# Forgetting attention in three steps a head instead of four: the first two query tiles share a step

## The chip, the cores and the metric

The kernel runs on one core of a Trainium2 chip. The metric is the device time of one execution in microseconds (us), lower is better. Engines are named as in the profile: PE is TensorE's matmul stream and PEld its weight loads, DVE is VectorE, ACT is ScalarE, POOL is GpSimd, and SPq is the SyncE queue that issues most transfers. Engines run side by side, each through its own instructions strictly in order, and wait for each other on semaphores.

## The reference, cut to what matters

The program is one step of a hybrid decoder: a combined projection, four branches (A to D), a merge, cross-attention over a memory and a feed-forward part, for 512 prompt tokens and 8 single-token samples. The change touches branch D for the prompt alone: causal attention with a forget gate, 8 heads of width 64, 512 queries in four tiles of 128.

```python
ck = jnp.swapaxes(c_k, 1, 2)[:, :, None, :]          # c = cumsum(log f)
def block(args):                                      # one tile of 128 queries
    qi, ci, pi = args
    s = jnp.einsum('bqhd,bkhd->bhqk', qi, k, preferred_element_type=F32) * (d ** -0.5)
    s = s + jnp.swapaxes(ci, 1, 2)[..., None] - ck
    s = jnp.where(k_pos[None, None, None, :] <= pi[None, None, :, None], s, NEG_INF)
    p = jax.nn.softmax(s, axis=-1)
    return jnp.einsum('bhqk,bkhd->bqhd', p.astype(v.dtype), v)
```

Query tile q sees q + 1 blocks of 128 keys, so its logits are 128, 256, 384 or 512 columns wide for q = 0 to 3. For the samples the same branch reads 128 pages of 256 KB of cached values (`cache_fox_v`), which is work of its own beside the prompt's.

## The kernel before, in words

All large products run as "pieces": 128 output columns of a weight matrix by all 520 tokens, in two halves of 260 tokens (`h` = 0 and 1). A half piece is 24 PE instructions (8 blocks of contraction, 3 products each for precision) or, for the `br` kinds (branch outputs, contraction 512), 12. Everything else is hung between half pieces. The function `timeline` writes one list of events for all engines, and each engine walks it and does its part of every event:

- `("piece", p, h)`: PE's half piece. With h = 0, SP issues the weights of piece p + 4, ACT and then POOL or DVE split those of piece p + 2 in a high and a low part.
- `("side", K, s)`: one step of the list `SIDE`, exactly one after each half piece, unless a `BEFORE` mark makes `through` put all steps up to that mark out in a row.
- `("evac", m)`: the finished tile m is taken out of PSUM by ACT or DVE.
- `("v", g)` and `("vx", b)`: a group of four cached value pages, multiplied on PE (`v_group`), and after each fourth group the sum over heads (`v_heads`), which needs a product that DVE makes first (L2067, waiting for the group) and a copy by DVE after it (L2071). At `("v", g)` SP issues the four pages of group g + 1 once group g - 1 has been used. `("PAGES",)` puts out all groups still open, one behind the other.

An attention step `("fox", n)` is a stage of a pipeline over n. Its PE part computes the logits of tile n into bank s0, transposes the exponentials of tile n - 1 into s1, and multiplies those of tile n - 2 with V into s2. Its DVE part, which comes first, takes the row maximum of tile n - 1's logits (L1790) and divides the result of tile n - 3 by its row sum (the reciprocal L1795, then a product recorded at L1599). Its ACT part copies the transposes out (L1380) and makes the exponentials (L1388), after DVE's maximum. Before PE starts its part of step n it waits until DVE and ACT have finished theirs of step n (L967 and L969); DVE and ACT wait for PE's part of step n - 1. So a step's DVE work is hidden only as far as PE has a half piece or a value group to run between its parts of step n - 1 and n:

```python
                done = K if kind == "y" else K + 1
                if upto(act_works, done):
                    pe.wait_ge(act_s.sem, upto(act_works, done))
                if upto(dve_works, done):
                    pe.wait_ge(dve_s.sem, upto(dve_works, done))
```

Pieces 82 to 95 (kinds `brB`, `gateB`) and 96 (`gateD`) run beside these steps. Before piece 97 the mark `("BEFORE", "brD")` puts out all attention steps and value groups that are left, then `("df", 1)`, which finishes the samples' part of branch D. After that `("split", "brD")` lets ACT write the high part of the branch's result (`oh`), and six export steps `("ex", n)` and the load of the cross-attention memory (`ml`) follow.

Of the kernel before, what the change touches and what calls it, by code (L numbers as in the profile page):

```python
# [18 lines left out]
ACT = mybir.ActivationFunctionType  # L19
AX = mybir.AxisListType.X  # L20
MUL, ADD, SUB, MAX, MIN = ALU.mult, ALU.add, ALU.subtract, ALU.max, ALU.min

P = 128
# [5 lines left out]
QT = SEQ // P  # L29
# [4 lines left out]
FH, FD = 8, 64  # L34
# [122 lines left out]
    return max(p for p, x in enumerate(PIECES) if x[3] == kind)  # L157


FOX = 4 * FH  # L160
XU = QT * XH // 2
VG = 4

# [283 lines left out]
def build(nc, a, out):  # L447
    ctx = ExitStack()
    with ctx:
# [25 lines left out]
        OD, OB, OC, QKV, G, DEC = 0, 2080, 4160, 6240, 12480, 18624  # L475
        DEC_N = 4 * 512 + 512 + PAGES * NB * FH
        SQ = DEC + DEC_N
# [6 lines left out]
        def v(at, *shape):  # L484
            n = int(np.prod(shape))
            x = ar[:, at:at + n]
            if len(shape) == 2:
                x = x.rearrange("p (a b) -> p a b", a=shape[0])
            if len(shape) == 3:
                x = x.rearrange("p (a b c) -> p a b c", a=shape[0], b=shape[1])  # L490
            return x

        oD, oB, oC = v(OD, KB, T), v(OB, KB, T), v(OC, KB, T)
        qkv = v(QKV, 12, T)
        fq, fk, fv = oD, qkv[:, 4:8, :], qkv[:, 8:12, :]
# [30 lines left out]
        bias = small(20)  # L526
        eps6, eps5 = small(1), small(1)
        dcol, edc, edl, kdf, bed = (small(16) for _ in range(5))
        nmx, rsum = small(2), small(2)
# [13 lines left out]
        s0, s1, s2, s3 = (sd[:, n, :] for n in range(4))  # L543
# [16 lines left out]
        pool_c, act_c, dve_c = stage("pool_chain"), stage("act_chain"), stage("dve_chain")  # L560
# [5 lines left out]
        pe_s, act_s, dve_s = stage("pe_side"), stage("act_side"), stage("dve_side")  # L566
        v2a, a2v = stage("dve_to_act"), stage("act_to_dve")
# [30 lines left out]
        wsl = nc.alloc_sbuf_tensor_at("wsl", [P, KD, 16], F32R, offset=base + 4 * (G + 256))  # L598
        zrow = v(G + 1024, T)
        vt = v(G, QT, 4 * 192)  # L600
        fP, fPT, frs = v(G + 3072, 512), v(G + 3584, QT, P), v(SQ, P)
        stg = v(G + 4096, 2, 512)

        cnh = nc.alloc_sbuf_tensor_at("cnh", [P, 512], F32R, offset=base + 4 * (G + 5632))
# [36 lines left out]
        def sel(h):  # L641

            return mask_r[0:NB, 0, h:h + 1].to_broadcast([NB, P])
# [190 lines left out]
        def _(pe):  # L834
            def mm(o, l, r, start=True, stop=True):
                return pe.matmul(o, l, r, start=start, stop=stop, skip_group_check=True)  # L836
# [114 lines left out]
            def side(K, s):  # L951
# [60 lines left out]
                    last = mm(s1[:, 32:64], cs(I_HI), f)  # L1012
                elif kind == "fox":
                    if n < FOX:
                        h, q = divmod(n, QT)
                        r = slice(FD * (h % 2), FD * (h % 2) + FD)
                        w = (q + 1) * P
                        mm(s0[:, 0:w], fq[r, h // 2, q * P:(q + 1) * P], fk[r, h // 2, 0:w], True, False)
                        mm(s0[:, 0:w], sel(h), cnh[0:FH, 0:w], False, False)
                        mm(s0[:, 0:w], sel(h), cnl[0:FH, 0:w], False, False)  # L1020
                        last = mm(s0[:, q * P:w], mask_r[:, 0, :], mask_r[:, 1, :], False, True)
                    if 1 <= n <= FOX:
                        for b in range((n - 1) % QT + 1):
                            last = tr(s1[:, b * P:(b + 1) * P], fP[:, b * P:(b + 1) * P])
                    if 2 <= n <= FOX + 1:
                        h, q = divmod(n - 2, QT)
                        for b in range(q + 1):
                            last = mm(s2[:, 0:P], vt[:, b, 192 * (h // 2) + FD * (h % 2):192 * (h // 2) + FD * (h % 2) + 2 * FD], fPT[:, b, :], b == 0, b == q)
                elif kind == "l2p":
                    for j in range(2):  # L1030
                        for h in range(2):
# [156 lines left out]
        def _(act):  # L1188
# [118 lines left out]
            def side(K, s):  # L1307
# [8 lines left out]
                fins = None  # L1316
# [58 lines left out]
                elif kind == "fox":  # L1375
                    if n == 1:
                        act.wait_ge(ss_st, 32)
                    w = ((n - 2) % QT + 1) if 2 <= n <= FOX + 1 else 1
                    if 2 <= n <= FOX + 1:
                        fins = act.activation(fPT[:, 0:w, :], s1[:, 0:w * P].rearrange("p (a b) -> p a b", a=w), ACT.Copy)  # L1380
                    else:
                        fins = act.activation(rsum[:, 1:2], eps6[:, 0:1], ACT.Copy)
                    if n <= FOX:
                        act_c.by(fins)
                        w = ((n - 1) % QT + 1) * P
                        act.wait_ge(v2a.sem, va + 1)
                        act.wait_ge(act_c.sem, act_c.n)
                        fins = act.activation(fP[:, 0:w], s0[:, 0:w], ACT.Exp, bias=nmx[:, 0:1])  # L1388
                elif kind == "l2":
                    if n == 0:  # L1390
                        act.wait_ge(qs_out, 16)
# [201 lines left out]
        def _(dve):  # L1593
            def own(ins, st=dve_c):
                st.by(ins)
                dve.wait_ge(st.sem, st.n)

            def tt(o, x, y, op, st=dve_c):
                own(dve.tensor_tensor(o, x, y, op), st)  # L1599
# [136 lines left out]
            def side(K, s):  # L1736
# [49 lines left out]
                    tt(cnl[0:FH, :], cneg[0:FH, :], cnh[0:FH, :].bitcast(F32), SUB, dve_s)  # L1786
                elif kind == "fox":
                    if n <= FOX:
                        w = ((n - 1) % QT + 1) * P
                        v2a.by(dve.tensor_reduce(nmx[:, 0:1], s0[:, 0:w], AX, MAX, negate=True))  # L1790
                    if n >= 3:
                        h, q = divmod(n - 3, QT)
                        r = slice(FD * (h % 2), FD * (h % 2) + FD)
                        rs_ = slice(FD - FD * (h % 2), 2 * FD - FD * (h % 2))
                        own(dve.reciprocal(frs[r, :], s2[rs_, 0:P]))  # L1795
                        tt(oD[r, h // 2, q * P:(q + 1) * P], s2[r, 0:P], frs[r, :], MUL, dve_s)
                    else:
                        fin()
                elif kind == "l2":
# [307 lines left out]
```

## Time and profile before

| | before |
|---|---|
| median of 3 runs | 1736.78 us (1733.03 to 1740.67) |
| the profiled execution, its own time | 1732.22 us |
| its span, first to last instruction | 1729.2 us |
| PE busy, share of the span | 1486.3 us, 86% |
| DVE, ACT, POOL busy | 961.7, 556.1, 563.1 us |
| mean granted TensorE clock | 0.923 of full speed |

PE is the engine that works most, and most of what it does is pieces; the attention steps and value groups between 805 and 1029 us are a part in which it also waits. All positions are microseconds from the start of the span. The granted clock is a share of full speed (1.00 is 2.4 GHz, 0.50 is 1.2 GHz).

### The profile page before, as it was taken

How to read it: one execution, taken by the hardware profiler on the slowest of the kernel's cores; microseconds unless marked ns; L12 is line 12 of the kernel's file. 1: busy time of each engine (PE TensorE's matmuls, PEld its weight loads, DVE VectorE, ACT ScalarE, POOL GpSimd, SP SyncE). 2: the span in 40 equal slices, each digit the busy share in tenths (PEclk: the TensorE clock that was granted, in tenths of full speed). 3: DMA queues.
4: the chain of work that ended last, by engine and by line, in shares of the span. 5: the costliest groups of instructions: out<-in, count | busy, mean ns of one | idle time of the engine just before them, and what ended most of it. 6: DMA issues, size and time to landing. Idle time of an engine off the chain costs nothing. (4 is left out here: it accounts for less than half of the span.)

```text
span 1729.2 us, 28170 instructions
## 1 busy us (share of the span) xinstructions
PE 1486.3 (86%) x11055; PEld 1379.2 (80%) x11055; DVE 961.7 (56%) x1366; ACT 556.1 (32%) x858; POOL 563.1 (33%) x311
## 2 busy tenths in 40 slices
PE   5986878688887989789888879898669999999995
PEld 5886877688887989766666658898558999999995
DVE  3189896899968675533223332265246777772212
ACT  5322650212133222534222222355335223233222
POOL 3355453343442433011111103320504444443440
PEclk9988987899998999999888889999879999999997
DMA  7425432434442544258444436433323333332331
GB/s 201 130 68 145 118 115 68 131 90 116 123 128 86 147 116 129 68 164 256 125 134 134 128 103 201 130 86 103 127 69 104 89 95 95 90 98 71 101 92 50
DMA packets 254643, 199.83 MB, mean 116 GB/s; under 512 B 15780, under 2 KB 212957, under 8 KB 254104
## 3 DMA queue, kind: packets, MB, share of 16 engines
q1 hardware_dynamic: 234149, 169.47, 34.0%
q10 hardware_dynamic: 19371, 23.86, 4.2%
q0 software_dynamic: 992, 4.72, 0.8%
q8 instruction: 87, 1.43, 0.3%
q14 instruction: 44, 0.36, 0.1%
HBM read 187.89 MB, written 10.81 MB: 115 GB/s over the span
## 5 line engine op out<-in xcount | busy, mean ns | idle before, releaser
L836 PE MATMUL pb<-xh,wh 128*128 128x260 f32 x2176 | 642.0, 295 | 34.1 <-ACT ar L1195 16.6
L836 PE MATMUL pb<-xl,wh 128*128 128x260 f32 x2176 | 628.7, 289 | 0.0
L836 PE MATMUL pb<-xh,rawl 128*128 128x260 f32 x2176 | 627.1, 288 | 0.0
L790 POOL TENSOR_TENSOR rawl<-raw,wh 128x1024 fp32r<-128x1024 f32 (+2 forms) x152 | 343.9, 2263 | 859.1 <-ACT wh L1195 858.5
L836 PEld LDWEIGHTS pb<-xh,wh 128*128 128x128 f32 x2176 | 425.1, 195 | 42.0 <-issue 28.7
L836 PEld LDWEIGHTS pb<-xl,wh 128*128 128x128 f32 x2176 | 425.3, 195 | 0.5
L836 PEld LDWEIGHTS pb<-xh,rawl 128*128 128x128 f32 x2176 | 424.7, 195 | 0.0
L1195 ACT ACTIVATE wh<-raw 128x1024 fp32r<-128x1024 f32 (+2 forms) x208 | 201.6, 969 | 513.1 <-PE pb L836 463.3
L836 PE MATMUL sd<-ar 128*128 128x128 f32 (+7 forms) x1488 | 258.8, 390 | 95.9 <-DVE ar L1599 63.3
L836 PEld LDWEIGHTS sd<-ar 128*128 128x128 f32 (+4 forms) x1488 | 177.2, 192 | 141.5 <-issue 85.0
L805 POOL TENSOR_TENSOR ar<-ar 128x512 f32<-128x512 f32 x128 | 191.1, 1493 | 249.0 <-DMA ar<-in_cache_fox_k 226.7
L836 PE MATMUL pb<-oh,wh 128*128 128x260 f32 (+1 forms) x384 | 120.6, 314 | 7.4 <-ACT ar L1195 5.4
L1727 DVE SCALAR_TENSOR_TENSOR ar<-xT,cols,ar 128x512 f32<-128x512 f32 x120 | 125.2, 1081 | 1.2
L836 PE MATMUL pb<-ol,wh 128*128 128x260 f32 (+1 forms) x384 | 114.5, 298 | 0.0
L836 PE MATMUL pb<-oh,rawl 128*128 128x260 f32 (+1 forms) x384 | 114.3, 298 | 0.0
L1710 DVE TENSOR_TENSOR rawl<-raw,wh 128x1024 fp32r<-128x1024 f32 (+1 forms) x56 | 67.1, 1199 | 75.4 <-ACT wh L1195 75.3
L840 PE MATMUL sd<-cst,ar 128*128 128x128 f32 (+6 forms) x363 | 63.7, 291 | 48.9 <-ACT ar L1505 20.7
L836 PE MATMUL pb<-hh,wh 128*128 128x260 f32 x352 | 100.0, 284 | 2.6 <-DVE hl L1599 2.6
L836 PE MATMUL pb<-hh,rawl 128*128 128x260 f32 x352 | 99.5, 283 | 0.0
L836 PE MATMUL pb<-hl,wh 128*128 128x260 f32 x352 | 99.3, 282 | 0.0
L1619 DVE SCALAR_TENSOR_TENSOR ar<-ar,cols 128x512 f32<-128x512 f32 x88 | 96.7, 1099 | 4.2 <-ACT ar L1195 2.6
L1734 DVE TENSOR_REDUCE ar<-ar 128x8 f32<-128x512 f32 x128 | 85.0, 679 | 23.1 <-POOL ar L805 22.1
(193 smaller groups left out, 1693.0 us busy)
## 6 DMA issues: line engine op xcount, KB each, us to landing
raw<-in_w_in SPq DMA_DIRECT2D x80, 512.0 KB, 4.2
ar<-in_cache_fox_k SPq DMA_DIRECT2D x128, 256.0 KB, 2.7
ar<-in_cache_fox_v SPq DMA_DIRECT2D x128, 256.0 KB, 3.1
raw<-in_w_ffn_in SPq DMA_DIRECT2D x44, 512.0 KB, 3.7
raw<-in_w_branch SPq DMA_DIRECT2D x32, 256.0 KB, 3.2
raw<-in_w_ffn_out SPq DMA_DIRECT2D x16, 512.0 KB, 3.9
ar<-in_cache_mem_k ACTq DMA_DIRECT2D x1, 4096.0 KB, 19.7
raw<-in_w_out SPq DMA_DIRECT2D x8, 512.0 KB, 3.9
```

The source lines that it names most:

```text
L790: pool.tensor_tensor(rawl[:, p % RING, 0:kt, :], raw[:, p % RING, 0:kt, :], wh[:, p % (AHEAD + 1), 0:kt, :].bitcast(F32), SUB).then_inc(lo ...
L805: own(pool.tensor_tensor(kring[:, i % 4, :], kring[:, i % 4, :], qb[:, :], MUL), prod_done)
L836: return pe.matmul(o, l, r, start=start, stop=stop, skip_group_check=True)
L840: return pe.transpose(o, i, ident[0:n, 0:n])
L1195: own(act.activation(o, i, f, **kw), st)
L1619: (st if j == width - 2 else dve_c).by(dve.scalar_tensor_tensor(out=y[:, 0:SEQ], in0=x[:, 4 - width + j:4 - width + j + SEQ], scalar=wcol( ...
L1710: dve.tensor_tensor(rawl[:, p % RING, 0:kt, :], raw[:, p % RING, 0:kt, :], wh[:, p % (AHEAD + 1), 0:kt, :].bitcast(F32), SUB).then_inc(lo. ...
L1727: dve_c.by(dve.scalar_tensor_tensor(out=oC[:, c, 0:SEQ], in0=g[:, j - 1:j - 1 + SEQ], scalar=w[:, j - 1:j], in1=oC[:, c, 0:SEQ], op0=MUL, ...
L1734: page_free.by(dve.tensor_reduce(sc[:, i, :], kring[:, i % 4, :].rearrange("p (h d) -> p h d", h=FH), AX, ADD))
```

## The change

Query tiles 0 and 1 (128 and 256 keys, together 384 columns) are put side by side in bank s0 and go through one step; tiles 2 and 3 keep a step each. A head takes three steps, and there are 27 attention steps in place of 35. The two tiles keep a row maximum and an exponential each; their three transposes are copied out at once; their results lie side by side in s2 (256 columns), and one reciprocal and one product, twice as wide, divide them.

```diff
-FOX = 4 * FH
+FOX = 3 * FH
+FOX_Q = ((0, 1), (2,), (3,))
+
+
+def fox_blocks(n):
+
+    return [(j, q, b) for j, q in enumerate(FOX_Q[n % 3]) for b in range(q + 1)]
...
-        fP, fPT, frs = v(G + 3072, 512), v(G + 3584, QT, P), v(SQ, P)
+        fP, fPT, frs = v(G + 3072, 512), v(G + 3584, QT, P), v(SQ, 2 * P)
...
-                        h, q = divmod(n, QT)
+                        h, at = n // 3, 0
                         r = slice(FD * (h % 2), FD * (h % 2) + FD)
-                        w = (q + 1) * P
-                        mm(s0[:, 0:w], fq[r, h // 2, q * P:(q + 1) * P], fk[r, h // 2, 0:w], True, False)
...
+                        for q in FOX_Q[n % 3]:
+                            w = (q + 1) * P
+                            o = s0[:, at:at + w]
+                            mm(o, fq[r, h // 2, q * P:(q + 1) * P], fk[r, h // 2, 0:w], True, False)
+                            mm(o, sel(h), cnh[0:FH, 0:w], False, False)
+                            mm(o, sel(h), cnl[0:FH, 0:w], False, False)
+                            last = mm(s0[:, at + q * P:at + w], mask_r[:, 0, :], mask_r[:, 1, :], False, True)
+                            at += w
                     if 1 <= n <= FOX:
-                        for b in range((n - 1) % QT + 1):
+                        for b in range(len(fox_blocks(n - 1))):
                             last = tr(s1[:, b * P:(b + 1) * P], fP[:, b * P:(b + 1) * P])
...
+                        for i, (j, q, b) in enumerate(fox_blocks(n - 2)):
+                            last = mm(s2[:, j * P:(j + 1) * P], vt[:, b, vs], fPT[:, i, :], b == 0, b == q)
...
+                        for j, q in enumerate(FOX_Q[(n - 1) % 3]):
+                            w = (q + 1) * P
+                            if j:
+                                act_c.by(fins)
+                            fins = act.activation(fP[:, at:at + w], s0[:, at:at + w], ACT.Exp, bias=nmx[:, j:j + 1])
+                            at += w
...
-                        w = ((n - 1) % QT + 1) * P
-                        v2a.by(dve.tensor_reduce(nmx[:, 0:1], s0[:, 0:w], AX, MAX, negate=True))
+                        qs, at = FOX_Q[(n - 1) % 3], 0
+                        for j, q in enumerate(qs):
+                            w = (q + 1) * P
+                            (v2a if j == len(qs) - 1 else dve_c).by(
+                                dve.tensor_reduce(nmx[:, j:j + 1], s0[:, at:at + w], AX, MAX, negate=True))
+                            at += w
                     if n >= 3:
-                        h, q = divmod(n - 3, QT)
+                        h, qs = (n - 3) // 3, FOX_Q[n % 3]
+                        w = len(qs) * P
...
-                        own(dve.reciprocal(frs[r, :], s2[rs_, 0:P]))
-                        tt(oD[r, h // 2, q * P:(q + 1) * P], s2[r, 0:P], frs[r, :], MUL, dve_s)
+                        own(dve.reciprocal(frs[r, 0:w], s2[rs_, 0:w]))
+                        tt(oD[r, h // 2, qs[0] * P:qs[0] * P + w], s2[r, 0:w], frs[r, 0:w], MUL, dve_s)
```

No half piece, value group or export step is added or taken away, and PE's products are the same ones. The list of events is the same up to the event `("v", 26)` behind piece 96, h = 0; what differs before it is only which tiles a step n handles. Behind it the order changes. PE's instructions from there to piece 97, before (`8x512` are the value groups, `128x1` their sums over heads, `sd<-cst,ar 128x128` transposes, `sd<-ar 128x128` the products with V, `pb` the pieces):

```order
4514 L836 MATMUL sd<-ar 8x512 x4
4515 L836 MATMUL sd<-ar 128x128
4516 L836 MATMUL sd<-cnh,mask_r 128x128
4517 L836 MATMUL sd<-cnl,mask_r 128x128
4518 L836 MATMUL sd<-mask_r 128x128
4519 L840 MATMUL sd<-cst,ar 128x128 x4
4520 L836 MATMUL sd<-ar 128x128 x3
4521 L836 MATMUL sd<-cst,ar 128x1 x4
4522 L836 MATMUL sd<-ar 128x256
4523 L836 MATMUL sd<-cnh,mask_r 128x256
```

This is value group 27, attention step 28, the sum over heads and the start of step 29; steps 30 to 33 with value groups 28 to 31 between them follow, and then piece 97. In the changed kernel PE has this between the two halves of piece 96 (the first two rows end half 0, the last two begin half 1):

```order
4498 L842 MATMUL pb<-xl,wh 128x260
4499 L842 MATMUL pb<-xh,rawl 128x260
4500 L842 MATMUL sd<-ar 8x512 x8
4501 L842 MATMUL sd<-cst,ar 128x1 x4
4502 L842 MATMUL sd<-ar 8x512 x16
4503 L842 MATMUL sd<-cst,ar 128x1 x4
4504 L842 MATMUL pb<-xh,wh 128x260
4505 L842 MATMUL pb<-xl,wh 128x260
```

All attention steps stand ahead of it, and value groups 26 to 31 stand in a row with nothing between them. On DVE, around the copy behind a sum over heads (step 12, beside piece 88), before:

```order
610 L2071 COPY ar<-sd 128x4
611 L1790 TENSOR_REDUCE ar<-sd 128x1
612 L1795 RECIPROCAL ar<-sd 64x128
613 L1599 TENSOR_TENSOR ar<-sd,ar 64x128
614 L1790 TENSOR_REDUCE ar<-sd 128x1
```

and in the changed kernel:

```order
610 L2091 COPY ar<-sd 128x4
611 L1808 TENSOR_REDUCE ar<-sd 128x1
612 L1815 RECIPROCAL ar<-sd 64x256
613 L1614 TENSOR_TENSOR ar<-sd,ar 64x256
614 L1808 TENSOR_REDUCE ar<-sd 128x1 x2
```

Steps whose number is a multiple of three now carry the wide reciprocal and product, and the step behind each carries two maxima.

## Rows read from the trace of the kernel before

Rows of stretches give: from:to and length in us; busy us and instructions of PE, PEld, DVE, ACT and POOL; the granted clock; the DMA share and GB/s. Timeline rows give start, length, engine, line and instruction, in brackets the idle time before and what ended it. Groups give count, busy us, mean ns of one, idle us before.

**Rows 1.** Stretches: steps beside pieces, the tail, and one slow stretch

```profile
805.30:989.20 183.90, 163.84 (x980) 123.39 (x984) 59.07 (x104) 40.89 (x74) 25.33 (x14) 0.84 0.46 136
989.20:1029.30 40.10, 30.76 (x169) 18.52 (x168) 13.04 (x22) 7.06 (x14) 1.26 (x1) 0.79 0.43 126
913.00:930.00 17.00, 14.66 (x63) 12.93 (x63) 4.91 (x10) 2.99 (x6) 2.45 (x2) 0.60 0.02 5
```

**Rows 2.** Who waited for whom from 805.3 to 1029.3 us: total, times, longest

```profile
PE sd L836 <- DVE ar L1599: 26.1, 12, 2.9
```

**Rows 3.** Timeline, two steps that PE waited for: behind a value group, behind sums

```profile
913.29 0.76 PE L836 MATMUL sd<-ar 64*128 64x128 f32 x2 [2.88 <-DVE ar L1599]
...
922.67 0.74 PE L836 MATMUL sd<-ar 64*128 64x256 f32 x2 [2.05 <-DVE ar L1599]
```

**Rows 4.** Groups of DVE instructions by shape: count, busy us, mean ns, idle before

```profile
L1795 DVE RECIPROCAL ar<-sd 64x128 f32<-64x128 f32 x32 | 30.6, 955 | 3.6 <-PE sd L836 2.6
L1599 DVE TENSOR_TENSOR ar<-sd,ar 64x128 f32<-64x128 f32 x32 | 9.2, 289 | 1.1
L1790 DVE TENSOR_REDUCE ar<-sd 128x1 f32<-128x512 f32 x8 | 5.5, 689 | 19.3 <-PE sd L836 19.3
L1790 DVE TENSOR_REDUCE ar<-sd 128x1 f32<-128x384 f32 x8 | 4.5, 558 | 23.4 <-PE sd L836 23.4
L1790 DVE TENSOR_REDUCE ar<-sd 128x1 f32<-128x256 f32 x8 | 3.4, 422 | 16.9 <-PE sd L836 14.3 <-PE sd L840 2.6
L1790 DVE TENSOR_REDUCE ar<-sd 128x1 f32<-128x128 f32 x8 | 2.3, 290 | 15.5 <-PE sd L836 15.4
...
L1950 DVE RECIPROCAL ar<-ar 128x64 f32<-128x64 f32 x1 | 0.6, 552 | 0.0
```

**Rows 5.** PE's part of a step, one stretch for each width, and the last step

```profile
900.60:902.50 1.90, 1.90 (x12) 1.06 (x9) 0.00 (x0) 0.32 (x1) 1.51 (x1) 1.00 0.64 195
905.10:907.70 2.60, 2.60 (x15) 1.42 (x12) 0.00 (x0) 0.00 (x0) 0.00 (x0) 1.00 0.77 215
942.00:944.00 2.00, 2.00 (x19) 1.78 (x16) 0.00 (x0) 0.00 (x0) 1.21 (x1) 1.00 0.90 227
948.00:950.20 2.20, 2.20 (x18) 1.69 (x15) 0.00 (x0) 0.00 (x0) 0.00 (x0) 1.00 0.35 111
1025.30:1026.50 1.20, 1.20 (x13) 1.06 (x9) 0.00 (x0) 0.00 (x0) 0.00 (x0) 0.90 0.00 0
```

**Rows 6.** Timeline, a step that hides behind a half piece and a value group

```profile
860.29 0.29 DVE L1790 TENSOR_REDUCE ar<-sd 128x1 f32<-128x128 f32 x1 [2.58 <-PE sd L836]
...
862.54 0.29 PEld L836 LDWEIGHTS sd<-ar 64*128 64x128 f32 x2 [0.86 <-issue]
```

**Rows 7.** Timeline of PE, from value group 25 to piece 97

```profile
979.46 0.67 PE L836 MATMUL sd<-ar 64*128 64x256 f32 x2 [0.41 <-DVE ar L1599]
...
983.20 1.89 PE L836 MATMUL sd<-ar 128*8 128x512 f32 x10
...
989.16 2.10 PE L836 MATMUL sd<-ar 128*8 128x512 f32 x10
...
995.76 1.04 PE L836 MATMUL sd<-ar 128*8 128x512 f32 x8
...
1001.79 1.71 PE L836 MATMUL sd<-cst,ar 128*128 128x1 f32 x8
...
1029.34 0.37 PE L836 MATMUL pb<-xh,wh 128*128 128x260 f32 x1
```

**Rows 8.** Value pages: SP's timeline (start, length, issues), and from issue to landing

```profile
976.21 3.63 SPq L728 DMA_DIRECT2D ar<-in_cache_fox_v  x4
...
985.01 35.44 SPq L728 DMA_DIRECT2D ar<-in_cache_fox_v  x20
...
ar<-in_cache_fox_v SPq DMA_DIRECT2D x93, 256.0 KB, 3.0
```

**Rows 9.** Timeline of ACT behind the last attention step

```profile
1031.63 2.65 ACT L1195 ACTIVATE oh<-ar 128x520 fp32r<-128x520 f32 x4 [3.48 <-DVE cols L1608]
```

More of the change, by code:

```diff
@@ L1014, in side @@
                     if n < FOX:
-                        h, q = divmod(n, QT)
+                        h, at = n // 3, 0
                         r = slice(FD * (h % 2), FD * (h % 2) + FD)
-                        w = (q + 1) * P
-                        mm(s0[:, 0:w], fq[r, h // 2, q * P:(q + 1) * P], fk[r, h // 2, 0:w], True, False)
-                        mm(s0[:, 0:w], sel(h), cnh[0:FH, 0:w], False, False)
-                        mm(s0[:, 0:w], sel(h), cnl[0:FH, 0:w], False, False)
-                        last = mm(s0[:, q * P:w], mask_r[:, 0, :], mask_r[:, 1, :], False, True)
+                        for q in FOX_Q[n % 3]:
[6 more added lines that the diff above has]
+                            at += w
                     if 1 <= n <= FOX:
-                        for b in range((n - 1) % QT + 1):
+                        for b in range(len(fox_blocks(n - 1))):
                             last = tr(s1[:, b * P:(b + 1) * P], fP[:, b * P:(b + 1) * P])
                     if 2 <= n <= FOX + 1:
-                        h, q = divmod(n - 2, QT)
-                        for b in range(q + 1):
-                            last = mm(s2[:, 0:P], vt[:, b, 192 * (h // 2) + FD * (h % 2):192 * (h // 2) + FD * (h % 2) + 2 * FD], fPT[:, b, :], b == 0, b == q)
+                        h = (n - 2) // 3
+                        vs = slice(192 * (h // 2) + FD * (h % 2), 192 * (h // 2) + FD * (h % 2) + 2 * FD)
+                        for i, (j, q, b) in enumerate(fox_blocks(n - 2)):
+                            last = mm(s2[:, j * P:(j + 1) * P], vt[:, b, vs], fPT[:, i, :], b == 0, b == q)
                 elif kind == "l2p":
@@ L1377, in side @@
                         act.wait_ge(ss_st, 32)
-                    w = ((n - 2) % QT + 1) if 2 <= n <= FOX + 1 else 1
+                    w = len(fox_blocks(n - 2))
                     if 2 <= n <= FOX + 1:
@@ L1384, in side @@
                         act_c.by(fins)
-                        w = ((n - 1) % QT + 1) * P
                         act.wait_ge(v2a.sem, va + 1)
                         act.wait_ge(act_c.sem, act_c.n)
-                        fins = act.activation(fP[:, 0:w], s0[:, 0:w], ACT.Exp, bias=nmx[:, 0:1])
+                        at = 0
+                        for j, q in enumerate(FOX_Q[(n - 1) % 3]):
[4 more added lines that the diff above has]
+                            at += w
                 elif kind == "l2":
@@ L1788, in side @@
                     if n <= FOX:
-                        w = ((n - 1) % QT + 1) * P
-                        v2a.by(dve.tensor_reduce(nmx[:, 0:1], s0[:, 0:w], AX, MAX, negate=True))
+                        qs, at = FOX_Q[(n - 1) % 3], 0
[4 more added lines that the diff above has]
+                            at += w
                     if n >= 3:
-                        h, q = divmod(n - 3, QT)
+                        h, qs = (n - 3) // 3, FOX_Q[n % 3]
+                        w = len(qs) * P
                         r = slice(FD * (h % 2), FD * (h % 2) + FD)
                         rs_ = slice(FD - FD * (h % 2), 2 * FD - FD * (h % 2))
-                        own(dve.reciprocal(frs[r, :], s2[rs_, 0:P]))
-                        tt(oD[r, h // 2, q * P:(q + 1) * P], s2[r, 0:P], frs[r, :], MUL, dve_s)
+                        own(dve.reciprocal(frs[r, 0:w], s2[rs_, 0:w]))
+                        tt(oD[r, h // 2, qs[0] * P:qs[0] * P + w], s2[r, 0:w], frs[r, 0:w], MUL, dve_s)
                     else:
```

## The prediction

> **What bounds the kernel now.** I read the busy shares of the page first, then PE's timeline of branch D. Over the whole program PE is the engine that works most, and wherever pieces run back to back nothing but PE's work counts. The attention steps lie in one part, which I cut in two: from step 0's start at 805.3 us to value group 26 at 989.2 us, where a half piece stands between any two steps, and the tail from there to piece 97 at 1029.3 us, where apart from the second half of piece 96 none does [rows 1]. PE has 20.1 us of idle time in the first stretch and 9.3 us in the tail, and runs at a mean clock of 0.84 and 0.79 in them. The table of waits says who it waits for: 26.1 us in 12 waits for DVE's product that ends a step [rows 2]. These waits are not spread evenly. All but a few stand behind a fourth value group (DVE must first do its head product, L2067, and only then the step) or behind a sum over heads (DVE's copy L2071 first). Two of them are 2.88 and 2.05 us [rows 3]. In all other steps a half piece and mostly a value group hide DVE: in one of them DVE starts at 860.29 and PE at 862.54, with PE never idle [rows 6]. So PE's time here is its own work, plus the waits at fixed places, plus a slower clock behind such waits (0.60 from 913 to 930 us [rows 1]). The number of steps as such costs PE next to nothing.
>
> **The change, part by part.** Between the start of step 0 and value group 26 there are 27 half pieces in either kernel, and a step after each but the last. Before, these slots take steps 0 to 26 of the 34 that have PE work; in the changed kernel they take all (0 to 25). I work out five terms.
>
> A, work moved into the first stretch. PE's part of a step took 2.0, 2.2, 1.9 and 2.6 us for steps whose number leaves 0, 1, 2 and 3 after division by four (the stretches from 942, 948, 900 and 905 us [rows 5]). Steps 27 to 33 go forward: 2.6 + 2.0 + 2.2 + 1.9 + 2.6, and the last two, without logits, 1.2 each (the last of [rows 5], for both). That is 13.7 us more before value group 26, and nothing hides it, since PE is what sets the pace there. I count no saving for eight fewer steps: the PE instructions are the same, and the slots between pieces remain.
>
> B, DVE's longer chain where PE already waits. A step's DVE work is the maximum of the tile before (0.29, 0.42, 0.56 or 0.69 us), a reciprocal of 0.955 and a product of 0.289 [rows 4]. The wide reciprocal of 256 is in no row. It can't be below the 0.96 of 128 columns nor, by proportion, above 1.91; between 64 and 128 columns the reciprocal grew by 0.403, 6.3 ns a column, which gives 0.955 + 128 x 0.0063 = 1.76, and I take that. The product of 256 I take as 0.42, adding the 0.13 that a maximum grows by from 128 to 256 columns [rows 4]. Going through the eight stalled steps of this stretch (5, 6, 10, 12, 16, 17, 22, 23) with the tiles that they now handle: steps 6 and 12 have the wide pair, where PE waits 1.2 and 0.95 us longer; steps 10, 16 and 22 get the two maxima of the merged tiles (0.29 + 0.42 + a gap of 0.03, for 0.42, 0.69, 0.42): 0.3, 0.05 and 0.3; steps 5 and 17 get 384 columns for 128: 0.27 each; step 23 stays. Sum 3.4 us. Queued behind the waiting PE step are the half piece and the value group after it, so all of this counts.
>
> C, steps that were hidden. With 12 instructions of a `br` half piece and a value group, PE came to its next step 2.25 us after DVE had begun, so some 2.1 us of DVE work fit [rows 6]; without the group's 1.04 us [rows 7] it is 1.2. The wide chain is 0.69 + 1.76 + 0.42 and gaps = 2.9 us. It sits in such a slot in steps 9 and 15: 0.8 us each. Step 18 has a `br` half piece alone: 1.8 us at full clock, less if the slow clock behind step 17 stretches the half piece; I take 1.2. Step 25 loses its maximum, as no logits come before it, and with it the wait of 0.41 us that it had [rows 7]. Steps 3 and 21 have 24 instructions and a group before them, 24 behind the slow clock; they stay hidden. Sum 2.4 us. The doubled exponential stays behind DVE's reciprocal and costs nothing; if it didn't, it would be the sum of two short ACT operations against one, under half a microsecond in each of eight steps.
>
> D, the tail. It took 40.2 us (989.16 to 1029.34 [rows 7]). In the changed kernel no step is left there, but neither is what hid the value pages. A group's four pages are issued 1.10 us apart ((3.63 - 0.34) / 3, if an issue itself takes 0.34 [rows 8]), so 4.4 us a group, and the last lands 3.0 us after its issue [rows 8]. Let value group 26 start at 0. Group 25 then started at -4.0: 1.04 for itself and 3.0 for the half piece, which is what 983.20 to 989.16 leaves beside the group and a step of 1.9 [rows 5, 7]. Group 27's pages are issued 1.8 us after that start (985.01 against 983.20 [rows 7, 8]), at -2.2, and land at 4.1. Groups 28, 29, 30 and 31 are issued from 2.2, 6.6, 11.0 and 15.4 on, by SP's pace alone, and land 3 x 1.10 + 3.0 = 6.3 later: 8.5, 12.9, 17.3, 21.7. Group 31 takes PE 1.04 us at full clock [rows 7] and, as the waits leave PE idle most of the time, likely nearly twice that, 1.9. DVE's head product over 512 columns (some 0.7, like a maximum of that width [rows 4]) with its hand-over, 1.0, and the sum over heads, 1.7 [rows 7], end the row at 26.3. The second half of piece 96 follows, 3.0 us at full clock and 6.0 at half; starting at half, 4.7. That is 31.0 us; at full clock throughout it is 21.7 + 1.0 + 1.0 + 1.0 + 3.0 = 27.7. I take 31.0: minus 9.2 us. The 13.7 of A leave the tail, but 4.5 of it comes back as waiting for pages.
>
> E, behind the tail. Before, piece 96 was complete ahead of the tail, so ACT had taken its tile out by the time piece 97 began, and started the four `oh` parts, 2.65 us together, 2.3 us after that [rows 7, 9]. Now piece 96 ends only behind the tail, and taking out its tile and the 2.65 stand between its end and ACT's first export copy, which PE's second export step needs, with one half piece of 3.0 for cover. I put 1.5 us, between 0 and 2.5.
>
> The sum: 13.7 + 3.4 + 2.4 - 9.2 + 1.5 = 11.8 us. The profiled execution took 1732.2 us of its own time with a span of 1729.2, so it would be 1744.0. That execution lies 4.6 us under the median of the runs shown, 1736.8; on the median the sum gives 1748.6, and I forecast 1748. About 0.5% or 8.7 us is what a measurement of this kernel can tell from no change: 1728.1 to 1745.5.
>
> **A rule weighed.** The Trainium skill (VectorE: DVE Perf Modes, on the TRN2 errata) says that VectorE pays a fixed cost per instruction and that one large tile pays it once where many small ones pay each. The maxima agree: 290 ns for 128 columns and 689 for 512 leave 157 ns that don't depend on width [rows 4]. By that rule alone 16 fewer instructions save 2.5 us and the kernel would come out 2.5 us faster, 1734. The saving is real on DVE, which is 56% busy; PE waits for it only at the places above, and there the merged step puts more in one wait and less in another, with both inside B and C.
>
> **The rivals.** (1) Little of B and C is seen and the tail runs at full clock: that is 13.7 + 3.4 + 0 - 12.5 + 0 = 4.6 us, 1741, no change that can be told. For it: the tail's clock rose again at times (group 27 took 1.04 at 995.76 [rows 7]). Against: pages come only every 4.4 us there. (2) The slow clock goes away, and the kernel is faster. The first stretch lost 0.16 of 183.9 us to the clock, 29 us, of which some 5 fell on idle time [rows 1]. Denser steps behind a wait (2.8 us of PE work on average for 2.2) could bring TensorE back to 2.4 GHz sooner. To reach minus 0.5% it must give back 11.8 + 8.7 = 20.5 of those 24 us; with all of them the time is 1725. Against it: the waits before the slow stretches do not get shorter, two of them grow by about 1 us. (3) The reverse: the new waits of 0.8 to 1.2 us in steps 9, 15 and 18 fall into stretches that ran at 2.4 GHz and pull the clock to 1.2 there. Three stretches of 5 us more at half clock cost 7.5 us: 1756. For it: such a wait stands one or two steps before one of 3 us. Against: the wait of 0.41 us at 979.46 changed nothing. (4) If the time hung on the number of steps, eight fewer at their mean distance of 6.6 us (224.0 us for 34 steps) would save 53 us; the slots without PE idle time speak against it, and I give it nothing of its own.
>
> The Trainium skill (TensorE: Matmul & The Clock Gate, Part 1) has the clock fall after idle time of PE and return after sustained work. By this rule the tail with 20 us of sparse value groups runs at the low level; the trace agrees so far as 913 to 930 us lay behind waits.
>
> **How the numbers follow.** The forecast gets 0.54, with a range of its own of 1743 to 1755: from D's full clock and E at 0 (plus 7.0) to wide reciprocals of 1.91 in six waits (0.9), E at 2.5 (1.0) and 4 us more of slow clock (plus 17.7). Rival 1 gets 0.23, rival 3 0.13, rival 2 0.10. The range of 1735 to 1758 leaves out rival 2 and the upper part of rival 3. Slower by over 0.5%: four fifths of the forecast's case, all of rival 3 and a little of rival 1, 0.58. Within 0.5%: 0.32. Faster: 0.10.
>
> **What would show it.** A: 26 steps of mean 2.8 us PE work before value group 26, and that group some 19 us later after step 0's start than the 183.9. B and C: reciprocals of 64x256 near 1.76 us; waits near 3.4 us at steps 6 and 12 and near 0.8 at 9 and 15. D: value groups 28 to 31 about 4.4 us apart, each ended by a DMA wait, and 31 us from group 26 to piece 97. E: a wait of PE for ACT's copy before the second export step. It would be wrong if the half-clock stretches shrank, if pages landed faster than SP's pace, or if PE's part of a merged step were shorter than the two it replaces.

## The result and the profile after

The changed kernel is slower: 1758.13 us, median of 4 runs (1755.49 to 1759.28), against 1737.0 us for the kernel before beside it; the ratio is 1.0122, 95% interval 1.0103 to 1.0142. That is 21 us. The profiled execution took 1757.97 us of its own time, 25.8 more than that of before. From the page of the changed kernel, the span and the busy times of the engines:

```profile
span 1756.2 us, 28112 instructions
PE 1508.7 (86%) x11055; PEld 1390.2 (79%) x11055; DVE 959.9 (55%) x1350; ACT 553.7 (32%) x850; POOL 560.6 (32%) x311
```

PE has the same 11055 instructions and is busy 22 us longer: most of the loss is PE's own work done more slowly, not waits. The stretches of the changed kernel that answer to [rows 1] (step 0 to value group 26; the tail to piece 97; piece 97 to the place in the order of pieces where the row of before below ends):

```profile
804.70:1016.80 212.10, 186.65 (x1060) 138.34 (x1064) 65.30 (x105) 44.48 (x78) 25.30 (x14) 0.82 0.40 116
1016.80:1044.90 28.10, 23.15 (x93) 6.99 (x93) 4.38 (x13) 0.07 (x1) 0.00 (x0) 0.94 0.61 182
1044.90:1078.70 33.80, 26.95 (x192) 25.93 (x190) 8.49 (x13) 12.17 (x22) 7.93 (x5) 0.85 0.56 185
```

and the kernel before in the third of them, which was not needed for the prediction:

```profile
1029.30:1056.40 27.10, 23.61 (x194) 22.35 (x194) 8.65 (x20) 11.10 (x20) 7.89 (x4) 1.00 0.46 149
```

The first stretch grew by 28.2 us (183.90 to 212.10), the tail shrank by 12.0 (40.10 to 28.10), and the part behind it grew by 6.7 (27.10 to 33.80). That is 22.9 of the 27.0 us between the two spans (1756.2 - 1729.2); the rest is 4.7 us behind these stretches and 0.6 less ahead of them, where the kernels are the same. In the first stretch PE's idle time went from 20.1 us (183.90 - 163.84) to 25.4 (212.10 - 186.65), 5.4 more. The other 22.8 are busy time, and the same stretch cut by output tile shows whose (`pb` are the pieces; `sd` the attention steps and value groups). Before, `pb` first and `sd` second:

```profile
805.30:989.20 183.90, 75.14 (x480) 70.17 (x480) 5.57 (x8) 3.62 (x6) 0.84 0.46 136
805.30:989.20 183.90, 98.22 (x500) 56.05 (x504) 47.31 (x86) 25.26 (x53) 0.84 0.46 136
```

After, in the same order:

```profile
804.70:1016.80 212.10, 74.91 (x480) 70.22 (x480) 4.87 (x7) 3.62 (x6) 0.82 0.40 116
804.70:1016.80 212.10, 121.24 (x580) 70.87 (x584) 55.41 (x89) 28.66 (x56) 0.82 0.40 116
```

(The two overlap in time, so they add up to more than PE's busy time.) The pieces cost the same in sum, the steps and groups 23.0 us more. The 80 PE instructions moved in were priced at 13.7 us at full clock, which leaves 9 us. The granted clock has two levels, so a mean of 0.84 says that 2 x 0.16 x 183.9 = 59 us were at the lower one, and 0.82 over 212.1 us that 76 were. Seventeen us more at half clock cost some 8.5 us of busy time, by this estimate nearly all of the 9. The waits of PE in the changed kernel from 804.7 to 1078 us (in total, times, longest), to set beside [rows 2]:

```profile
PE sd L842 <- DVE ar L1614: 25.4, 11, 3.4
PE sd L846 <- DMA ar<-in_mem_prompt: 3.6, 1, 3.6
PE sd L846 <- ACT ar L1480: 3.1, 2, 2.3
PE sd L842 <- DMA ar<-in_cache_fox_v: 2.9, 6, 1.2
```

The wait for DVE's product is as large as before in sum, but all of it now stands in the first stretch (before it was 20.0 us in 9 waits there). The waits for the value pages are new, and those for ACT's export copy are longer: before they are 0.61 and 0.51 us, at the third and the fifth export step. DVE's groups, beside [rows 4]:

```profile
L1815 DVE RECIPROCAL ar<-sd 64x128 f32<-64x128 f32 x16 | 15.3, 955 | 2.9 <-PE sd L842 2.4
L1815 DVE RECIPROCAL ar<-sd 64x256 f32<-64x256 f32 x8 | 14.0, 1756 | 0.2
...
L1614 DVE TENSOR_TENSOR ar<-sd,ar 64x256 f32<-64x256 f32 x8 | 3.4, 422 | 0.3
```

Both sizes that no row of before had came out as estimated (1.76 and 0.42 us).

Two places in PE's timeline of the changed kernel, steps 15 and 16 and then step 18, show what the added waits do:

```profile
923.50 0.46 PE L842 MATMUL sd<-ar 64*128 64x128 f32 x2 [0.76 <-DVE ar L1614]
...
926.13 1.08 PE L846 MATMUL sd<-cst,ar 128*128 128x128 f32 x4
927.00 1.49 PE L842 MATMUL sd<-ar 128*128 128x128 f32 x6
928.14 0.57 PE L842 MATMUL pb<-oh,wh 128*128 128x260 f32 x1
...
931.02 1.47 PE L842 MATMUL sd<-ar 128*8 128x512 f32 x8
935.30 0.95 PE L842 MATMUL sd<-ar 64*128 64x384 f32 x1 [2.82 <-DVE ar L1614]
...
954.61 0.46 PE L842 MATMUL sd<-ar 64*128 64x128 f32 x2 [1.25 <-DVE ar L1614]
...
957.60 1.07 PE L846 MATMUL sd<-cst,ar 128*128 128x128 f32 x4
958.47 1.49 PE L842 MATMUL sd<-ar 128*128 128x128 f32 x6
959.61 0.57 PE L842 MATMUL pb<-xh,wh 128*128 128x260 f32 x1
```

Step 15 waits 0.76 us, and its PE part, from 923.50 to 928.14, takes 4.6 us; the half piece of 12 behind it, to 931.02, takes 2.9, where 1.6 is its time at full clock. Step 18 waits 1.25 us and takes 5.0. A merged step's PE part takes 3.3 us where the clock is full, as in step 9 of this kernel. The tail, PE's timeline again, beside [rows 7]:

```profile
1016.77 1.04 PE L842 MATMUL sd<-ar 128*8 128x512 f32 x8
1019.04 3.01 PE L842 MATMUL sd<-ar 128*8 128x512 f32 x8 [1.22 <-DMA ar<-in_cache_fox_v]
...
1037.96 1.85 PE L842 MATMUL sd<-ar 128*8 128x512 f32 x4 [0.24 <-DMA ar<-in_cache_fox_v]
1040.67 1.05 PE L842 MATMUL sd<-cst,ar 128*128 128x1 f32 x8 [0.85 <-DVE ar L2087]
1041.58 0.36 PE L842 MATMUL pb<-xh,wh 128*128 128x260 f32 x1
...
1044.55 0.60 PE L846 MATMUL sd<-cst,ar 128*11 128x128 f32 x4
...
1050.33 0.61 PE L846 MATMUL sd<-cst,ar 128*11 128x128 f32 x4 [2.30 <-ACT ar L1480]
...
1070.16 3.64 PE L846 MATMUL sd<-cst,ar 128*128 128x128 f32 x16 [3.60 <-DMA ar<-in_mem_prompt]
```

PE follows the value pages one by one, with short waits, and the mean clock is 0.94: it is 0.51 from 1024.0 to 1027.5 us and 1.00 in the rest of the tail. The last four pages are worked off by 1039.8, 23.0 us behind the start of group 26 (23.6 was predicted), and half 1 of piece 96 takes 3.0 us, which is full clock. Behind it stand two waits, for ACT's copy and for the memory's rows, each with half clock after it. Of the 6.7 us by which the third stretch grew, 3.4 are idle time (27.10 - 23.61 before, 33.80 - 26.95 now) and 3.3 busy time.

### The profile page after: what moved, and what is told of

Read it like the earlier page. It is cut to its first block and busy times, and to the rows that moved or that the text cites. A ratio compares the mean times of both kernels' runs of the same rounds, so it can differ in the third digit from the quotient of the medians.

```text
span 1756.2 us, 28112 instructions
## 1 busy us (share of the span) xinstructions
PE 1508.7 (86%) x11055; PEld 1390.2 (79%) x11055; DVE 959.9 (55%) x1350; ACT 553.7 (32%) x850; POOL 560.6 (32%) x311
## 5 line engine op out<-in xcount | busy, mean ns | idle before, releaser
L842 PE MATMUL sd<-ar 128*128 128x128 f32 (+7 forms) x1488 | 273.8, 394 | 98.8 <-DVE ar L1614 62.5
L842 PEld LDWEIGHTS sd<-ar 128*128 128x128 f32 (+4 forms) x1488 | 182.7, 196 | 150.3 <-issue 83.3
```

## The experiments

Eight kernels ran in two sets, each set beside runs of the kernel before. Differences between kernels are taken from their ratios, in shares of 1737 us.

**1 and 2. DVE's samples' work behind the next attention step, in either kernel.** Nearly all waits stand where DVE has a head product or a copy to do ahead of the step. Here DVE holds that work back until the next step is done; PE's order stays as it is.

```diff
+            held = []
+            def late():
+                while held:
+                    what, g = held.pop()
...
                 elif e[0] == "side":
+                    if e[2][0] != "fox":
+                        late()
                     side(e[1], e[2])
+                    late()
...
-                elif e[0] == "v" and e[1] % V_OF == V_OF - 1:
...
-                elif e[0] == "vx":
+                elif e[0] in ("v", "vx"):
+                    late()
+                    if e[0] == "vx" or e[1] % V_OF == V_OF - 1:
+                        held.append(e)
```

In the kernel before:

> The kernel before, with one change of order on DVE alone: the head product behind a fourth value group and the copy behind a sum over heads are made after the attention step that follows them in the list, not before it. Nothing else moves. If the 9 waits of 2 to 2.9 us in the first stretch (20 us) and the slow clock behind them (22 us over what the same PE instructions take at full clock) come from DVE's order, both go: the first stretch falls from 184 to about 145 us, the tail from 40 to about 33, and the kernel takes 1690 to 1700 us. If the clock does not depend on these waits, only they go: about 1717. If the value pages' transfers set the pace, under 5 us are gained: 1732 or more.

Measured: 1698.29 us (1688.54 to 1701.8), ratio 0.9784 (0.9752 to 0.9816). In the changed kernel:

> The same change of order in the changed kernel. With the waits gone, merging costs its moved PE work at full clock (14 us), the waits of the wide steps (about 4 us), and what follows the tail, less what the shorter tail gives back: 1708 to 1716 us, 12 to 20 us behind the kernel before with the same order. If the merged steps are themselves what slows the clock, it stays over 1725.

Measured: 1716.01 us (1707.58 to 1721.04), ratio 0.9887 (0.9852 to 0.9921). The stretches of the first (step 0 to group 26, and the tail):

```profile
804.30:949.00 144.70, 143.73 (x976) 106.69 (x976) 58.98 (x104) 40.95 (x74) 25.41 (x14) 0.96 0.59 172
949.00:984.10 35.10, 28.91 (x170) 17.82 (x169) 13.54 (x23) 7.08 (x14) 1.27 (x1) 0.85 0.50 146
```

and those of the second (first stretch and tail):

```profile
803.20:970.84 167.64, 164.28 (x1056) 123.24 (x1057) 65.67 (x105) 44.52 (x78) 25.33 (x14) 0.93 0.50 146
970.84:999.30 28.46, 22.91 (x92) 7.00 (x92) 4.29 (x13) 0.00 (x0) 0.00 (x0) 1.00 0.60 178
```

PE's waits for DVE's product in the second one's first stretch:

```profile
PE sd L842 <- DVE ar L1614: 3.3, 3, 1.7
```

In the kernel before, 19 us of waits in the first stretch took another 20 us with them: PE is busy 143.73 us there in place of 163.84, with the clock at 0.96 in place of 0.84. The time falls into the first range of its expectation, so the reading of the waits was right, and each microsecond of them costs about two. (The profiled execution is the fastest of its five, 9.8 us under their median; by the medians the gain is 38.7 us where the two profiled executions are 43.7 apart, so the exact factor is uncertain.) The change stays a loss of 17.9 us without the long waits, inside the 12 to 20 expected. The new waits of merged steps (0.76, 0.76 and 1.74 us, steps 9, 15 and 18) are the 3.3 that are left.

**3. The last eight steps back in the tail.** The changed kernel with eight empty places in `SIDE` ahead of step 0:

```diff
+        + [("SKIP",)] * 8
         + [("fox", n) for n in range(FOX + 3)]
```

> The changed kernel with eight slots left empty ahead of attention step 0. The last eight steps then stand in the tail again, among the value groups, as before, and piece 96 is complete ahead of the tail. Two of the fixed waits fall into empty slots and vanish. If the loss comes from where the work went (first stretch at slow clock, emptied tail, piece 96 behind it), the kernel is back at 1730 to 1740 us. If it comes from merging as such (wider DVE chains, longer PE parts), it stays over 1750.

Measured: 1742.27 us (1738.62 to 1747.33, 10 runs), ratio 1.0022 (1.0003 to 1.0041). This is 2.3 us above the first theory's range and 7.7 below the second's. 17 of the 21 us go away with the place of the steps, 4 stay. The tail of this kernel, from group 26 to piece 97, beside [rows 1]:

```profile
988.50:1035.60 47.10, 35.07 (x189) 22.15 (x187) 14.85 (x22) 7.87 (x15) 1.27 (x1) 0.78 0.34 101
```

It is 7.0 us longer than before (40.10): 4.3 of it busy time, since eight of 27 steps hold more of PE's work than eight of 35, and 2.7 idle time. Its waits there for DVE's product are 8.0 us in four and one of 3.2; the longest, 3.4 us, is again that of a wide division behind the copy of a sum over heads.

The place of the steps is not all that this run changes. As its expectation says, two of the fixed waits fall into empty slots. The waits for DVE's product ahead of group 26, first in the kernel before (805.3 to 989.2 us), then in this one (803 to 988.5):

```profile
PE sd L836 <- DVE ar L1599: 20.0, 9, 2.9
PE sd L848 <- DVE ar L1620: 16.1, 7, 3.4
```

So this kernel is spared 3.9 us of waiting that the kernel before has, with what clock hangs on it, and the 4 us that stay understate what merging costs.

**4. The same with the deferred DVE work**, to see merging without the long waits:

> The changed kernel with DVE's head product and copy made behind the next attention step, and eight empty places ahead of attention step 0, so that the last eight steps lie among the value groups behind piece 96 again, as they do in the kernel before. Against the kernel before with the same order on DVE (1698 us) only the merging is different. If the cost of the change is where the steps lie, this takes 1696 to 1703 us (1698, plus some 2 us of waits where a wide division has little to hide behind, give or take the cover of the pages). If merging itself costs, through longer chains of DVE, 1706 us or more. If the number of steps costs PE something, as the eight fewer would show here without the placement, 1693 us or less.

Measured: 1708.95 us (1698.47 to 1711.44), ratio 0.9832 (0.981 to 0.9853), 8.3 us behind experiment 1 and so in the range of the second theory: merging has a cost of its own. The two 95% intervals put it between 2 and 15 us. The tail of this kernel:

```profile
950.40:992.40 42.00, 33.71 (x188) 20.71 (x187) 15.94 (x24) 7.86 (x15) 1.26 (x1) 0.84 0.39 113
```

PE's waits for DVE's product in it:

```profile
PE sd L848 <- DVE ar L1620: 3.9, 3, 2.3
PE sd L852 <- DVE ar L1620: 3.2, 1, 3.2
```

and the same waits in the tail of the first kernel of experiments 1 and 2:

```profile
PE sd L836 <- DVE ar L1599: 2.8, 4, 1.1
PE sd L840 <- DVE ar L1599: 2.2, 1, 2.2
```

This tail takes 42.0 us for 35.1, which is most of the 10.7 us between the two spans (1696.7 and 1686.0), with 7.1 us of such waits for 5.0 and 4.8 us more of busy time. Each step follows the last there with only a value group between, and a wide division has less to hide behind. Of the busy time the rows don't separate what is the steps' larger share of PE's work, which the first stretch then has less of, and what is clock.

**5. Piece 96 complete ahead of the row of value groups.** One empty place ahead of the last value groups puts half 1 of piece 96 between groups 26 and 27, as it is before:

```diff
+        + [("SKIP",)] * 1
         + [("PAGES",), ("df", 1)] + [("BEFORE", "brD")]
```

> The changed kernel with one empty slot ahead of the last value groups, so that the second half of piece 96 stands between value groups 26 and 27 and the piece is complete before the tail. If 5 to 7 us are lost behind the tail because ACT's work on piece 96 starts late, they come back, and 2 to 3 us in the tail where the half piece covers a page transfer: 1749 to 1752 us. If what is lost behind the tail is the load of the cross-attention memory, under 3 us come back: 1755 or more.

Measured: 1751.7 us (1747.75 to 1754.96), ratio 1.0081 (1.0054 to 1.0108): 7 us back, the first range. PE's second export step in this kernel:

```profile
1052.60 0.60 PE L852 MATMUL sd<-cst,ar 128*11 128x128 f32 x4
```

and its stretch behind the first export step:

```profile
1049.60:1078.00 28.40, 25.28 (x211) 24.22 (x209) 7.89 (x12) 10.51 (x20) 7.88 (x4) 1.00 0.61 202
```

The wait of 2.30 us for ACT at the second export step is gone, that for the memory's rows is 1.66 us in place of 3.60, and the clock behind the first export step is 1.00, where it was 0.85. With the deferred DVE work as well:

> The changed kernel with DVE's head product and copy made behind the next attention step, and one empty place ahead of the last value groups, so that the second half of piece 96 stands between groups 26 and 27 and the piece is complete ahead of the tail. Without the deferred DVE work the same place gave 6.4 us. If the two causes are independent, it gives 5 to 7 us here too: 1709 to 1711 us. If the late half piece only cost time because the clock was low behind other waits, it gives 2 us or less: 1714 us or more.

Measured: 1704.5 us (1703.41 to 1706.1), ratio 0.9805 (0.9785 to 0.9826), 14 us below experiment 2, beyond the range. The spans of the two profiled executions differ by 4.9 us (1705.8 and 1700.9), and the runs of experiment 2 spread over 13 us. Group 26 to the end, the part in which the kernels differ, takes 4.0 us less (735.0 and 731.0). The first stretch is the same list of instructions in both. It takes 167.64 us in experiment 2, and here:

```profile
807.60:969.90 162.30, 158.15 (x1056) 116.81 (x1056) 68.23 (x107) 44.53 (x78) 25.32 (x14) 0.97 0.52 152
```

That is 5.3 us between two executions of the same instructions, with the same three waits of 3.3 us (and one more of 0.8 in the faster one) and a mean clock of 0.97 for 0.93. Behind the wait of 1.74 us at step 18 the clock was low in one (0.59 from 918.16 to 923.3 us) and full in the other (1.00 from 919 to 930 us). So with the deferred DVE work, differences of some 5 us in this stretch can't be put down to a change by one profile each; why the medians are 14 us apart stays open.

**6. The wide division cut to the width of one tile.** In a merged step the reciprocal and the product cover the first 128 columns, so that the second tile of each head stays undivided.

```diff
-                        own(dve.reciprocal(frs[r, 0:w], s2[rs_, 0:w]))
-                        tt(oD[r, h // 2, qs[0] * P:qs[0] * P + w], s2[r, 0:w], frs[r, 0:w], MUL, dve_s)
+                        own(dve.reciprocal(frs[r, 0:P], s2[rs_, 0:P]))
+                        tt(oD[r, h // 2, qs[0] * P:(qs[0] + 1) * P], s2[r, 0:P], frs[r, 0:P], MUL, dve_s)
```

> The changed kernel, but in a merged step DVE takes the reciprocal and the product of the first 128 of the two tiles' 256 columns alone (the second tile of each head stays undivided: this is left out), so DVE's chain there is as long as that of a single tile. Everything else, placement and PE's work, stays. If the added 21 us are work moved (14), longer waits (5.5) and the slow clock behind fresh waits, this gives back 5.8 us of waits (0.93 at steps 6 and 12 each, the 0.76 of steps 9 and 15, most of the 1.25 of step 18) and, if the slow clock behind steps 15 and 18 comes from these waits (rival 3 of the prediction), another 3 to 5 us: 1747 to 1751 us. If the slow clock has nothing to do with the new waits, 1752 to 1754 us. If the wide instructions cost nothing at all, no change from 1758.

Measured: 1746.98 us (1740.8 to 1752.66, 8 runs), ratio 1.0054 (1.0034 to 1.0073): 12 us back, at the edge of the first range (1747 to 1751). The first stretch of this kernel and its share of the steps and groups:

```profile
803.70:1004.90 201.20, 180.36 (x1057) 134.50 (x1057) 57.84 (x105) 44.55 (x78) 25.33 (x14) 0.85 0.42 121
803.70:1004.90 201.20, 117.04 (x577) 69.21 (x577) 47.95 (x89) 28.71 (x56) 0.85 0.42 121
```

It is 10.9 us shorter than the 212.10: 4.6 of idle time (25.4 to 20.8) and 6.3 of busy time, though PE does the same work. (In the first kernel of experiment 5, whose division is wide, this stretch takes 213.9 us and its steps 15 and 18 are as slow, 4.6 and 5.0 us.) Steps 15 and 18 in its timeline, the rows that answer to those above:

```profile
921.31 0.62 PE L846 MATMUL sd<-cst,ar 128*128 128x128 f32 x4
921.77 0.83 PE L842 MATMUL sd<-ar 128*128 128x128 f32 x6
...
948.13 0.62 PE L846 MATMUL sd<-cst,ar 128*128 128x128 f32 x4
948.60 0.83 PE L842 MATMUL sd<-ar 128*128 128x128 f32 x6
```

The same transposes take 0.62 us in place of 1.08, the same products 0.83 in place of 1.49. From step 15 to step 19 PE is busy 29.02 us here and 35.12 in the changed kernel, so that 6.1 of the 6.3 us lie there. So waits of 0.76 and 1.25 us, behind which the clock was at its lower level, cost some 6 us of slower work beside their own length. With the deferred DVE work as well:

> The changed kernel with both: DVE's head product and its copy behind the sums go behind the next attention step, and in merged steps DVE divides the first 128 columns only (the second tile of each head stays undivided: this is left out). Against the same kernel with the full division (1716 us) the waits of 0.76 at steps 9 and 15 and of 1.74 at step 18 must be gone: 3.3 us. If the slow clock behind step 18 there (PE's parts of 5.2 and 4.2 us) was caused by that wait, it goes too, another 4 to 6 us: 1707 to 1710 us. If the slow clock stays in its place, 1712 to 1714 us.

Measured: 1707.57 us (1705.48 to 1718.67, 4 runs), ratio 0.9838 (0.9798 to 0.9879), 8.5 us below experiment 2 by the ratios. Its first stretch:

```profile
803.20:965.54 162.34, 161.46 (x1054) 120.10 (x1054) 58.13 (x104) 43.70 (x78) 25.36 (x14) 0.94 0.50 149
```

and the waits for the product in it:

```profile
PE sd L842 <- DVE ar L1614: 0.8, 1, 0.8
```

That is 5.3 us shorter than the 167.64 of experiment 2. The 2.5 us of waits for the product (3.3 to 0.8) are what the narrow division gives. The 2.8 of busy time can't be put down to it, as the same stretch with the wide division also took 162.30 us (experiment 5), nor can the 8.5 us be told from no change: the intervals leave it open by 9 us either way, and the two spans differ by 0.5 us.

These profiles show one thing more: the clock also falls where PE did not wait. In the kernel of experiment 2 the PE parts of steps 6 and 12 take 4.28 and 4.03 us for 3.3, at a granted clock of 0.76 and 0.81, with no idle time of PE before them; eight matmuls of one column each (a sum over heads, 0.95 us) stand right ahead. In experiment 1 the same sums stand in a first stretch that has full clock from 815 us on. PE's busy time in this stretch grows from 143.73 us there to 161.46 here, 17.7 us where 13.7 were moved in, although there is but one wait of 0.8 us left. What brings the low clock there stays open.

## Why the prediction missed

It gave 1748 with a range of 1735 to 1758, and the time is 1758.13: the direction was right, the size 10 us too small. Point by point:

- **A, work moved (plus 13.7).** The work is there: 80 more PE instructions on `sd` in the first stretch. PE's busy time grew by 22.8. With the narrow division (experiment 6) it still grows by 16.5 (180.36 - 163.84), so 6.3 us of the excess of 9.1 go with the new waits and 2.8 do not. A was priced as if all of it ran at full clock, in a stretch whose mean was 0.84, at which 13.7 us of work would take 16.3. That fits, but no run shows it by itself, and with the old waits gone the moved work also took more than 13.7 (17.7, experiments 1 and 6).
- **B and C, waits (plus 5.8).** The idle time grew by 5.4 us: 3.0 at the eight stalled steps, where 3.4 were worked out, and 2.4 at the others, as worked out. The waits at steps 9, 15 and 18 are 0.76, 0.76 and 1.25, where 0.8, 0.8 and 1.2 were worked out, and the longest are 3.4 us as said. The sizes were right.
- **What C's waits do to the clock (rival 3, chance 0.13) is the step that failed.** The forecast held the mean clock, with at most 4 us more in its range, because a wait of 0.41 us had changed nothing. Rival 3 had waits of 0.8 to 1.2 us pull the clock down, for 7.5 us in three stretches, and gave 1756. Experiment 6 shows 6.3 us of it, in two places, steps 15 and 18: the forecast held a wait to cost its own length, and these cost more than that in the work behind them. Step 9 waits the same 0.76 us and has no slow clock behind it (its PE part takes 3.3 us), and in experiment 2 step 15 hasn't either, with the same wait; in the second kernel of experiment 5 even the 1.74 us of step 18 had none behind it. So the slow clock at steps 15 and 18 goes with the new waits, but such a wait does not always bring it; what else it takes stays open.
- **D, the tail (minus 9.2).** It gave 12.0. The pages' pace was right: 23.0 us to the last page where 23.6 was worked out. What was off is the clock. It was taken as half for group 31 and, to begin with, for the half piece behind it; it was 1.00 from 1027.5 us on, and half 1 of piece 96 took 3.0 us for 4.7. By the Trainium skill (TensorE: Matmul & The Clock Gate, Part 1) the clock falls after idle time of PE, and the prediction took PE to be idle for most of the tail. That premise is what failed: PE waits 0.2 to 1.2 us at a time and its records cover 23.15 of 28.10 us, so this tail is no test of that sentence. In this kernel's first stretch, waits of 2.3 to 3.4 us had the lower level behind them, which agrees with it.
- **E, behind the tail (plus 1.5, at most 2.5).** It is plus 6.7, the second term that was sized too small. The named wait came, 2.30 us for ACT's copy at the second export step. The term stopped there. Not counted were the half clock behind it (the next half piece takes 4.5 us for 3.0), 0.8 us at the fourth export step, and the memory's rows, for which PE now waits 3.60 us where it waited 2.17 before, again with half clock behind (0.51 from 1068.4 to 1075.3 us). Experiment 5 gives 7 us back by moving one half piece.

Summed over the profile: 28.2 - 12.0 + 6.7 = 22.9. The forecast's terms by the same cut were 19.5 - 9.2 + 1.5 = 11.8. The missing 11.1 are 8.7 of first stretch, by the estimate above nearly all clock, and 5.2 behind the tail, less 2.8 that the tail gave more.

The rule that the prediction weighed for DVE, that 16 fewer instructions save 2.5 us, is not borne out as a gain: DVE's busy time did fall, by 1.8 us (961.7 to 959.9), but the kernel became slower.

The wider theory, that placement and not merging makes the loss, holds in the main for the order of DVE that the kernel has (17 of 21 us, experiment 3, part of it two of the old waits that fall away with the empty slots). It does not hold in general: with the long waits removed, merging alone costs some 8 us (2 to 15, experiment 4). Rival 4, a saving by the number of steps, is refuted by the same two runs, in which eight fewer steps save nothing (plus 4 and plus 8 us). Rival 2 had the slow stretches shrink; they grew, from 59 to 76 us.

The best kernel is experiment 1, the kernel before with DVE's samples' work held back: 1698.29 us, 2.2% under before. Of the merged kernels the best is that with the deferred work and the early half piece, 1704.5.

## What to carry to other kernels

Where the granted clock of a stretch is under 1, a new wait may cost more than its length (6.3 us of slower work beside 4.6 of waits here): look what stands behind it, and price work moved into the stretch at the stretch's mean clock and not at the full one. Before merging steps of a pipeline to save instructions, ask which engine's chain a merged step lengthens and what hides it; here the engine that waited was the busy one, and the steps that were "saved" had been the cover for transfers. And look first for work of another stream that stands ahead of the critical chain on a half idle engine: moving that behind gave 38 us where the change that was under study lost 21.

## What the hardware showed beyond expectation

- Removing 19 us of PE waits returned another 20 us of PE busy time (163.84 to 143.73 us for the same stretch).
- Short waits between matmuls in the tail (0.2 to 1.2 us, 28 us long, PE busy 23.15) left the mean granted clock at 0.94, with one fall to the lower level from 1024.0 to 1027.5 us; in experiment 2, with such waits too, it was 1.00.
- The same list of instructions took 162.3 us in one execution and 167.6 in another, at a mean clock of 0.97 and 0.93, with the same three waits of 3.3 us for DVE's product (experiments 2 and 5).
- The clock fell with no idle time of PE ahead of it, behind eight one-column matmuls (steps 6 and 12 of experiment 2, 4.28 and 4.03 us for 3.3).
- The reciprocal on DVE goes on growing by the same 6.3 ns a column at twice the width of the rows of before: 955 ns for 128 columns and 1756 for 256. The multiplication grows by 133 ns for the same 128 columns (289 to 422).
